# A decoder layer's last two MLP blocks taken together, for half of the tokens at a time

## The reference, cut to what matters

```python
def squared_relu_mlp(x, w_up, w_down):
    return jnp.square(jax.nn.relu(x @ w_up)) @ w_down

# w_up is 1024 x 4096, w_down is 4096 x 1024
m = squared_relu_mlp(h, w_up[l], w_down[l])
h = layer_norm(DEEPNORM_ALPHA * h + m, ln3_g[l], ln3_b[l])
```

## Time and profile before

| what | value |
|---|---|
| device time, median of 3 | 1660.16 us |
| device time of the profiled execution | 1660.99 us |
| its span, first to last instruction | 1659.2 us |
| PE busy | 1530.4 us, 92% |
| DVE busy | 899.9 us, 54% |
| ACT busy | 465.6 us, 28% |
| POOL busy | 536.9 us, 32% |
| granted PE clock, mean | 0.957 |

### The profile page before, as it was taken

One profiled execution on the slowest core, in us unless ns is written; L12 is line 12 of the kernel. 1 busy time (PEld: TensorE's weight loads), 2 busy tenths in 40 slices (PEclk: granted clock), 3 DMA queues, 4 the chain that ended last, 5 costly groups with the idle time before them and its releaser, 6 DMA issues.

```text
span 1659.2 us, 20746 instructions
## 1 busy us (share of the span) xinstructions
PE 1530.4 (92%) x7720; PEld 1301.2 (78%) x7720; DVE 899.9 (54%) x1827; ACT 465.6 (28%) x987; POOL 536.9 (32%) x540
## 2 busy tenths in 40 slices
PE   7999966988878999989999999999999999999993
PEld 6887756887768998778887788888888888888872
DVE  7568986779786433593427633333333333333348
ACT  3015436788664651121301211111111111110110
POOL 5242215666410003342233343333333333333100
PEclk9999987999876999999999999999999999999997
DMA  5564324555400004311110211111111111110002
GB/s 221 180 185 144 122 76 150 171 164 158 129 25 15 13 12 160 96 50 40 50 52 0 102 58 44 51 51 51 52 51 51 52 51 51 51 52 26 1 0 101
DMA packets 61331, 128.96 MB, mean 78 GB/s; under 512 B 6960, under 2 KB 34096, under 8 KB 53552
## 3 DMA queue, kind: packets, MB, share of 16 engines
q1 hardware_dynamic: 44208, 100.37, 18.3%
q10 hardware_dynamic: 17024, 27.27, 4.6%
HBM read 100.35 MB, written 27.26 MB: 77 GB/s over the span
## 4 chain that ended last, share of the span: by engine, by line
PE 76%; DVE 15%; issue 3%; ACT 3%; POOL 1%; DMA 1%; ACTq 0%; SPq 0%; DVEq 0%; POOLq 0%
PE banks L647 22%; PE banks L649 21%; PE banks L648 21%; PE banks L840 3%; PE banks L699 2%; PE banks L700 2%; DVE unread L1443 2%; PE banks L827 2%; ACT unread_wide L1017 2%; DVE h_buf L1752 1%; PE banks L849 1%; DVE bn L1738 1%; PE banks L796 1%; DVE trial L1420 1%; DVE h_buf L1761 1%
## 5 line engine op out<-in xcount | busy, mean ns | idle before, releaser
L633 POOL TENSOR_SCALAR w_hi<-raw 128x512 fp32r<-128x512 f32 x268 | 174.9, 680 | 1021.8 <-PE banks L649 688.4
L638 POOL TENSOR_TENSOR w_lo<-raw,w_hi 128x512 fp32r<-128x512 f32 x268 | 364.7, 1395 | 0.0
L1863 DVE TENSOR_TENSOR h_buf<-h_buf,banks 128x1024 f32<-128x1024 f32 x120 | 146.5, 1221 | 146.5 <-PE banks L649 146.5
L647 PE MATMUL banks<-w_hi,hid_hi 128*128 128x512 f32 x512 | 200.9, 392 | 7.9 <-DVE h_buf L1863 7.9
L647 PE MATMUL banks<-act_hi,w_hi 128*128 128x512 f32 x512 | 199.9, 390 | 1.7 <-DVE act_lo L1731 1.7
L648 PE MATMUL banks<-w_lo,hid_hi 128*128 128x512 f32 x512 | 200.4, 391 | 0.0
L649 PE MATMUL banks<-w_hi,hid_lo 128*128 128x512 f32 x512 | 200.2, 391 | 0.0
L649 PE MATMUL banks<-act_hi,w_lo 128*128 128x512 f32 x512 | 199.9, 390 | 0.0
L648 PE MATMUL banks<-act_lo,w_hi 128*128 128x512 f32 x512 | 199.8, 390 | 0.0
L1233 ACT ACTIVATE relu_buf<-banks 128x512 f32<-128x512 f32 x64 | 38.3, 599 | 549.6 <-PE banks L649 549.6
L1827 DVE TENSOR_TENSOR relu_buf<-relu_buf 128x512 f32<-128x512 f32 x64 | 45.0, 705 | 249.6 <-ACT relu_buf L1233 249.6
(11 more groups left out here) (178 smaller groups left out, 2805.5 us busy)
## 6 DMA issues: line engine op xcount, KB each, us to landing
raw<-w_up_dram SPq DMA_DIRECT2D x16, 1024.0 KB, 4.8
raw<-w_down_dram SPq DMA_DIRECT2D x16, 1024.0 KB, 4.8
q_tile<-qk_dram SPq DMA_DIRECT2D x176, 64.0 KB, 2.2
qk_dram<-q_hi ACTq DMA_DIRECT2D x28, 256.0 KB, 2.3
qk_dram<-roped ACTq DMA_DIRECT2D x28, 256.0 KB, 2.7
x_raw<-x_t_dram SPq DMA_DIRECT2D x8, 512.0 KB, 8.4
raw<-wk_mem_dram SPq DMA_DIRECT2D x4, 1024.0 KB, 5.9
raw<-wv_mem_dram SPq DMA_DIRECT2D x4, 1024.0 KB, 5.0
```

Of the source, the lines that this page charges most:

```text
L633: pool.tensor_scalar(w_hi[s][:, col], raw[r % 2][:, col], 1.0, 1.0, ALU.mult, ALU.mult)\
L638: pool.tensor_tensor(w_lo[s][:, col], raw[r % 2][:, col], w_hi[s][:, col].bitcast(F32), ALU.subtract).then_inc(w_ready, 1)
L647: pe.matmul(dst, lh, rh, start=(first and n == 0), stop=False)
L1863: dve.tensor_tensor(h_buf[:, t, :], h_buf[:, t, :], ring_l[n % 2][:], ALU.add)\
```

## The change

Blocks f = 0 to 13 are left as they were (28 units). The last four units are reordered from (14, 0), (14, 1), (15, 0), (15, 1) to (14, 0), (15, 0), (14, 1), (15, 1), and the two units with the same tokens share one accumulation: `down_pair` runs, for each of four token tiles and each half of the output columns, the six matmuls of block 14 and then the six of block 15 into the same PSUM bank. DVE adds once for both (8 adds fewer), and then takes moments and norm. The `last_uses` entry of a w_up chunk now looks its unit up in the new order. The core of the diff:

```diff
+UNITS = [(f, hf) for f in range(N_FF - 2) for hf in range(2)]
+N_SINGLE = len(UNITS)
+UNITS += [(f, hf) for hf in range(2) for f in (N_FF - 2, N_FF - 1)]
...
-        last[C_MLP + 2 * f] = ("A", A_UP + 4 * f + 3)
-        last[C_MLP + 2 * f + 1] = ("L", L_DOWN + 8 * f + 7)
+        last[C_MLP + 2 * f] = ("A", A_UP + 2 * UNITS.index((f, 1)) + 1)
+        if f < N_FF - 2:
+            last[C_MLP + 2 * f + 1] = ("L", L_DOWN + 8 * f + 7)
...
+            def down_pair(u):
+
+                parts = []
+                for v in (u, u + 1):
+                    c = C_MLP + 2 * UNITS[v][0] + 1
+                    parts.append((hid_hi[v % 2], hid_lo[v % 2]) + tuple(parts_of(c, 2)))
+                    pe.wait_ge(w_ready, PIECES * c)
+                pe.wait_ge(hid_ready, 2 * u + 2)
+                for tt in range(4):
+                    n = L_DOWN + 4 * N_SINGLE + 4 * ((u - N_SINGLE) // 2) + tt
+                    freed(pe, l_free, n)
+                    tok = slice(tt * P, (tt + 1) * P)
+                    for half in range(2):
+                        col = slice(half * HALF, (half + 1) * HALF)
+                        for v, (hh, hl, wh, wl) in enumerate(parts):
+                            if tt == 0 and half == 0 and v == 1:
+                                pe.wait_ge(hid_ready, 2 * u + 4)
+                            mm = exact(ring_l[n % 2][:, col],
+                                       [(hh[:, j, tok], hl[:, j, tok], wh[:, j, col], wl[:, j, col])
+                                        for j in range(2)], first=(v == 0), final=(v == 1))
+                    mm.then_inc(l_full[n % 2], 1)
...
+            for u in (N_SINGLE, N_SINGLE + 2):
+                up(u + 1)
+                if u == N_SINGLE:
+                    up(u + 2)
+                down_pair(u)
...
@@ ACT
+            u = N_SINGLE + 2
+            for q in (2 * u, 2 * u + 1):
+                rectify(q)
+            for t in range(4):
+                root(2 * NT + t)
+            for q in (2 * u, 2 * u + 1):
+
+                filled(act, l_full, L_DOWN + 4 * N_SINGLE + 3)
+                round_hidden(q)
...
@@ DVE
+            for u in (N_SINGLE, N_SINGLE + 2):
+                for q in (2 * u + 2, 2 * u + 3):
+                    square(q)
+                    split_hidden(q)
+                if u == N_SINGLE:
+                    for q in (2 * u + 4, 2 * u + 5):
+                        square(q)
+                for tt in range(4):
+                    t = 2 * (u - N_SINGLE) + tt
+                    n = L_DOWN + 4 * N_SINGLE + t
+                    add_down(n, t, False)
+                    emptied(dve, l_free, n)
+                    moments(2 * NT + t, t)
+                    if u == N_SINGLE and tt == 3:
+                        for q in (2 * u + 4, 2 * u + 5):
+                            split_hidden(q)
+                    if t:
+                        norm(2 * NT + t - 1, t - 1)
```

More of the change, by code:

```diff
@@ L893, in up @@
             def up(u):
-                f, hf = divmod(u, 2)
+                f, hf = UNITS[u]
                 wh, wl = parts_of(C_MLP + 2 * f, NK)
@@ L959, in _ @@
                 turn_result(*transposed_at(g))
-            for u in range(2 * N_FF):
-                if u + 1 < 2 * N_FF:
-                    up(u + 1)
+            for u in range(N_SINGLE):
+                up(u + 1)
                 down(u)
+            for u in (N_SINGLE, N_SINGLE + 2):
+                up(u + 1)
+                if u == N_SINGLE:
+                    up(u + 2)
+                down_pair(u)
         @block.scalar
@@ L1247, in _ @@
                 round_hidden(q)
[L1248 to L1255, removed]
+            for u in range(N_SINGLE + 1):
+                for q in (2 * u + 2, 2 * u + 3):
[3 more added lines that the diff above has]
+            for q in (2 * u, 2 * u + 1):
+                rectify(q)
+            for t in range(4):
+                root(2 * NT + t)
+            for q in (2 * u, 2 * u + 1):
+                filled(act, l_full, L_DOWN + 4 * N_SINGLE + 3)
+                round_hidden(q)
+            for q in (2 * u + 2, 2 * u + 3):
+                rectify(q)
+                round_hidden(q)
+            for t in range(4, NT):
+                root(2 * NT + t)
         @block.vector
@@ L1839, in _, with add_down @@
                 split_hidden(q)
[L1840 to L1845, removed]
+            def add_down(n, t, first):
+                filled(dve, l_full, n)
+                if first:
+                    dve.wait_ge(ln_done, NT + t + 1)
+                    dve.scalar_tensor_tensor(out=h_buf[:, t, :], in0=h_buf[:, t, :], scalar=ALPHA,
+                                             in1=ring_l[n % 2][:], op0=ALU.mult, op1=ALU.add)\
+                        .then_inc(l_free[n % 2], 1)
+                else:
+                    emptied(dve, l_free, n - 8)
+                    dve.tensor_tensor(h_buf[:, t, :], h_buf[:, t, :], ring_l[n % 2][:], ALU.add)\
+                        .then_inc(l_free[n % 2], 1)
@@ L1846, in _ @@
+            for u in range(N_SINGLE):
+                square(2 * u + 2)
+                split_hidden(2 * u + 2)
+                square(2 * u + 3)
                 f, hf = divmod(u, 2)
                 for tt in range(4):
-                    if tt == 1 and more:
+                    if tt == 1:
                         split_hidden(2 * u + 3)
[L1851 to L1869, removed]
+                    add_down(L_DOWN + 4 * u + tt, 4 * hf + tt, f == 0)
+            for u in (N_SINGLE, N_SINGLE + 2):
+                for q in (2 * u + 2, 2 * u + 3):
+                    square(q)
[14 more added lines that the diff above has]
+                        norm(2 * NT + t - 1, t - 1)
```

## The result

Four runs of the changed kernel gave 1637.15 us in the median (1633.94 to 1642.59), four of the kernel before 1660.07 (1659.70 to 1660.46). The ratio is 0.9865, with a 95% interval of 0.9833 to 0.9898. The profiled execution took 1633.94 us, with a span of 1632.1.

A forecast was written before the change was run, and what follows sets the result against it. PE was taken to bound the kernel until 1608 us and DVE the tail. Four norms moved ahead, less a 1.75 us new wait, saved 16.3 us: 1660.16 - 16.3 = 1643.9 us, range 1642.1 to 1648.

The forecast's parts named there:

- What bounds the kernel: Whole span: PE bounds it until 1608 us, DVE after; DVE takes 5.85 us a tile against PE's 2.72.
- Four norms ahead, beside matrix work: Pair 28: tiles 0 to 3 get adds, moments and norms beside PE's work, with add(3) at 1595.4 us.
- The new wait: Pair 30's first tile: PE stalls after six matmuls for the last hidden part, costing 1.75 us in all.
- The sum: End of span: add(4) at 1612.6, add(7) at 1630.1, then 12.7 us, ending at 1642.9; 16.3 us less.
- The clock: Behind the new wait in pair 30: no fall of PE's clock assumed; one low stretch would cost 1.7 us.
- The range: Whole kernel: from 1642.1 us with no stall to 1648 us with the first rival and most of the second.
- The rivals: One clock fall (0.18), late hidden parts (0.10), late block 15 weights (0.03), clock low through pair 30 (0.05).
- The weights: Block 15's weight chunks, wanted earlier by pair 28, arrive late and make it slower, up to 1666 us; chance 0.03.
- the hidden parts: Before pair 30: the square of q = 62 slips behind norm(2), costing 2 to 5 us, 1646 to 1649; chance 0.10.

The follow-up runs named there:

- e_cover: Changed kernel with the first tile of each pair running block 14 for both output halves, then block 15; 1637.13 us, tail 36.3 us.
- e_nocover: Changed kernel with the wait for both hidden parts moved ahead of each pair's first matmul; 1641.71 us, tail 40.8 us.
- c_before: The kernel before, rerun with no edit; median 1655.30 us over 12 runs.
- c_after: The changed kernel, rerun with no edit; median 1637.30 us over 6 runs.
- c_before2: The kernel before, rerun once more with no edit; 1659.98 us in 1 run.
- c_after2: The changed kernel, rerun once more with no edit; median 1640.89 us over 6 runs.
- e_pool: e_cover with norms reordered in DVE's queue and the last pass of the norms of tiles 4, 5 and 6 on POOL; 1634.55 us, tail 36.8 us.

## Why the prediction was wrong

**What bounds the kernel**, and that only the DVE-bound tail counts: right. PE's four waits for DVE's adds, 7.9 us, are gone.

**Four norms ahead, beside matrix work**: right. Relative to the start of the tail, I had the adds of tiles 0 to 3 at -27.0, -21.6, -15.7 and -9.8 us. They came at -27.0, -21.6, -15.7 and -9.9.

**The new wait**: 1.7 us forecast for PE's delay, and an idle time of 1.5 as the records show it; it was 1.44. Add(4) was forecast 7.4 us into the tail and came at 7.4. Steps of 5.85 us after that: 5.86, 5.86 and 5.86. e_cover and e_nocover confirm that each microsecond of this wait is one of the end.

**The sum**: a tail of 37.7 us forecast, 37.6 to 37.7 in three traces. The gain of 16.3 us is that between the tails; the means of all runs, 16.2 apart, can bear it out only to about 3 us.

**The clock**: no fall behind the wait, as I took it. The price of a fall, about 1.7 us, was seen in e_nocover. The prediction compared the new gap with two gaps of before, of 2.35 and 1.49 us; a third one there, 2.84 us in front of the matmul at 1630.20, also had matmuls 0.43 us apart behind it. So in these traces gaps of 2.35, 2.84 and 3.03 us had a fall behind them, and gaps of 1.44 and 1.49 had none.

**The step that failed** is the last of the sum, "the median of the runs is 0.83 lower, which gives 1660.16 - 16.3 = 1643.9", and before it "Where PE isn't held up, pair 30 starts when down(30) did, at 1605.21". Both take the head of one trace as a constant of the program. It is not: pair 30 started at 1594.47, 1592.42 and 1602.08 in the three traces of the changed kernel, and the times of c_before and of c_after each move by 13.4 us with nothing changed. Three runs within 0.5 us of each other hid this. With the mean of the 59 runs in its place the same sum gives 1654.4 - 16.3 = 1638.1, where the changed kernel's mean is 1638.2 (that the two agree to 0.1 is luck, with 3 us of noise in the means). So the mechanism and its size were right, and the base was mis-sized, by 5.8 us. The cause stays open in one point: the four runs of the kernel before that stood beside the changed kernel did take 1660.07, and no run shows why those lay together at the long end.

**The range** failed with it. Its low end of 1642.1 rested on "below that the DVE chain would have to be shorter, which nothing offers". The DVE chain wasn't shorter, but the head was, in most runs: only 4 of the changed kernel's 16 runs took over 1642.1 us. What moves the head is the granted clock in the first 640 us, 0.91 in the mean of the trace of before. I had the row with its slices of 6 to 8 tenths and used it only to find where the tail begins. A clock that falls and comes back many times there is a term that can come out otherwise in every execution, on the fast side too.

**The rivals**: none of the four was it. The weights were never waited for, and the hidden parts weren't late.

The list lacked a rival, "the base is one draw". How far the clock of the first 640 us moves from run to run is seen in these rows of `c_before2` and `c_after`, whose heads are 1604.2 and 1592.4 us:

```profile
0.00:640.00 640.00, 548.00 (x3327) 0.91 0.37 120
```

```profile
0.00:640.00 640.00, 550.79 (x3394) 0.94 0.38 124
```

## What to carry to other kernels

Where a tail has one engine doing a fixed piece of work for each tile, finish some of the tiles early, beside the other engine's work, and bring the first of the rest forward; here the sum of the passes in that engine's queue, read from the rows of before, gave the length of the changed tail within 0.1 us. Take the base of a forecast from more than a few runs that agree, or widen the range by what the clock's slices leave open: where a stage shows a clock that falls and recovers, each execution can come out otherwise. And compare small edits by the stretch of the trace that they touch, since here a saving of 1.4 us was plain in the tail and lost in the times.

## What the runs showed of the hardware

The sparse attention stage, with its many products of 64 columns, can run at either clock, with PE busy in both: 134 matmuls in 17.1 us at 2.4 GHz, or 77 at 1.2 GHz, in the same program (c_after, c_after2). The low stretch lasted all of these 17.1 us although PE never idled in them, and in c_before it ended earlier. How busy PE was in 511.0 to 513.5 us did not tell these executions apart. With this stage and the ones around it, runs of one program spread over 14.6 us of 1654 (1648.4 to 1663.0).

A DVE pass over two SBUF tensors took 1.27 us alone and 2.85, 3.27 and 3.23 us when a POOL pass was under way (e_pool); one of one SBUF and one PSUM tensor kept its 1.22 us.
